# FFN down projection: resident activations loaded in half-width blocks, element-wise sums issued 4 to 11 units ahead

## The reference

```
def conv_ffn(h, w_up, conv_w, conv_b, w_down):
    u = h @ w_up                      # 1024 -> 2 * 2816
    u = centred width-3 depthwise convolution of u over tokens + conv_b
    g, val = jnp.split(u, 2, axis=-1)
    return (jax.nn.silu(g) * val) @ w_down      # 2816 -> 1024

x = x + g_f * f                       # f = conv_ffn(...), in layer()
```

## Time and profile before

| | us |
|---|---|
| median of three runs | 3349.37 |
| profiled execution: its own time | 3348.12 |
| profiled execution: span from first to last instruction | 3346.3 |
| PE busy in the span | 3166.0 (95%) |
| VectorE busy | 2230.3 (67%) |
| ScalarE busy | 1449.4 (43%) |
| down projection of layer 0 | from 1493.5 |
| down projection of layer 1 | from 3063.3 |

### The profile page before, as it was taken

How to read it: one execution, slowest core, us unless ns; L and a number is a source line. 1 busy time by engine, 2 the same in 40 slices (tenths; PEclk the granted TensorE clock), 3 DMA queues, 4 the chain that set the end, 5 groups by cost and what they waited for, 6 DMA issues and landing times. The chain is left out here.

```text
span 3346.3 us, 51277 instructions
## 1 busy us (share of the span) xinstructions
PE 3166.0 (95%) x20077; PEld 2922.7 (87%) x20077; DVE 2230.3 (67%) x3110; ACT 1449.4 (43%) x2665; POOL 985.3 (29%) x748
## 2 busy tenths in 40 slices
PE   6899999997989999999997999999898999999998
PEld 4788788886889999999997878787698999999998
DVE  5555566655166878777973566666518777877895
ACT  3344444444233333334553556665514333334453
POOL 1122222222346434420033122222136544442000
PEclk9999999998999999999999999999899999999999
DMA  6333344333222222239662111111332222225864
GB/s 237 106 102 110 106 124 117 98 103 137 95 70 66 79 73 66 73 106 326 201 189 69 42 31 33 29 30 38 120 114 71 66 73 72 73 73 167 283 202 159
DMA packets 287964, 362.09 MB, mean 108 GB/s; under 512 B 38836, under 2 KB 214061, under 8 KB 286573
## 3 DMA queue, kind: packets, MB, share of 16 engines
q1 hardware_dynamic: 268205, 294.06, 27.9%
q10 hardware_dynamic: 11664, 42.47, 3.9%
q0 software_dynamic: 7856, 22.29, 1.9%
HBM read 277.74 MB, written 67.37 MB: 103 GB/s over the span
## 5 line engine op out<-in xcount | busy, mean ns | idle before, releaser
L198 PE MATMUL psum<-Hh,wh 128*128 128x384 f32 x2048 | 706.8, 345 | 43.5 <-PEq L1018 12.5
L200 PE MATMUL psum<-Hl,wh 128*128 128x384 f32 x2048 | 692.6, 338 | 0.0
L199 PE MATMUL psum<-Hh,wl 128*128 128x384 f32 x2048 | 692.3, 338 | 0.0
L198 PEld LDWEIGHTS psum<-Hh,wh 128*128 128x128 f32 x2048 | 390.1, 190 | 58.6 <-issue 34.1
L1670 DVE SCALAR_TENSOR_TENSOR ff_c<-ff_u,par,ff_c 128x1153 f32<-128x1153 f32 x176 | 401.4, 2281 | 6.1
L199 PEld LDWEIGHTS psum<-Hh,wl 128*128 128x128 f32 x2048 | 390.3, 191 | 0.0
L200 PEld LDWEIGHTS psum<-Hl,wh 128*128 128x128 f32 x2048 | 389.6, 190 | 0.0
L1402 POOL TENSOR_TENSOR wl<-wr,wh 128x1024 fp32r<-128x1024 f32 x88 | 235.4, 2675 | 202.4 <-ACT wh L1201 202.4
L1402 POOL TENSOR_TENSOR ff_dl<-ff_dr,ff_dh 128x1024 fp32r<-128x1024 f32 x76 | 202.1, 2661 | 301.3 <-ACT ff_dh L1201 301.3
L2499 DVE TENSOR_REDUCE da_nb<-psum 128x1 f32<-128x1152 f32 x144 | 174.7, 1233 | 63.3 <-PE psum L2440 63.3
L3085 PE MATMUL psum<-ident,ga_e 128*128 128x128 f32 x1168 | 169.7, 286 | 22.8 <-ACT ga_e L2907 20.9
(11 more groups left out here) (342 smaller groups left out, 7615.9 us busy)
## 6 DMA issues: line engine op xcount, KB each, us to landing
wr<-w_up SPq DMA_DIRECT2D x88, 512.0 KB, 3.8
ff_dr<-w_down SPq DMA_DIRECT2D x130, 256.0 KB, 3.5
wr<-w_down SPq DMA_DIRECT2D x112, 256.0 KB, 3.6
act_save<-ff_c SPq DMA_DIRECT2D x44, 512.0 KB, 2.6
da_mw<-mod_w ACTq DMA_DIRECT2D x40, 512.0 KB, 3.9
wr<-mod_w ACTq DMA_DIRECT2D x40, 512.0 KB, 4.8
ff_c<-act_save SPq DMA_DIRECT2D x88, 192.0 KB, 3.8
wr<-w_qkv_diff SPq DMA_DIRECT2D x24, 512.0 KB, 18.3
```

The costliest lines, as they stand in the source:

```text
L198: pe.matmul(out, w_hi, m_hi, start=start, stop=False)
L199: pe.matmul(out, w_lo, m_hi, start=False, stop=False)
L200: return pe.matmul(out, w_hi, m_lo, start=False, stop=stop)
```

## The change

Three things change. The resident rows are loaded as blocks of 192 KB, in another order: blocks n = 1 of rows 4, 5, 6, 7 at step 7, of rows 0 to 3 and 8 to 10 at steps 17 to 23; blocks n = 0 of rows 0 to 10 at steps 24 to 29 (two in a step); blocks n = 0 of rows 11 to 21 at steps 30 to 40; blocks n = 1 of rows 11 to 21 at steps 45 to 55. Before the first block of the second and of the fourth group SP waits until the 11 blocks of the group before on the same semaphore have landed. P1 begins when the 11 blocks n = 1 of rows 0 to 10 are there. Then, the weight sum of unit q is issued in iteration q - 4 in place of q - 2, and the token sum in iteration q - 3 (P5), q - 6 (P6), q - 11 (P7) or q - 9 (P4). Last, the counts that ACT and DVE wait for follow the new order of sums (SUM_AT), and P2 waits for all blocks of rows1.

```diff
-ROWS_AT = {3: 4, 5: 5, 7: 6, 9: 7, 17: 0, 18: 1, 19: 2, 20: 3, 21: 8, 22: 9, 23: 10, 24: 11, 25: 12, 26: 13, 27: 14, 28: 15,
-           29: 16, 30: 17, 31: 18, 32: 19, 44: 20, 45: 21}
+ROWS_AT = {}
+for i, (row, n) in enumerate([(r, 1) for r in (4, 5, 6, 7, 0, 1, 2, 3, 8, 9, 10)]):
+    ROWS_AT[(4, 5, 6, 7, 17, 18, 19, 20, 21, 22, 23)[i]] = [(row, n)]
+for i in range(HALF):
+    ROWS_AT[24 + i // 2] = ROWS_AT.get(24 + i // 2, []) + [(i, 0)]
+    ROWS_AT[30 + i] = [(HALF + i, 0)]
+    ROWS_AT[45 + i] = [(HALF + i, 1)]
...
+W_LEAD, T_LEAD = 4, {"P5": 3, "P6": 6, "P7": 11, "P4": 9}
+SUM_ORDER = sorted([(q - W_LEAD, 0, q) for q in range(UNITS_DN) if down_name(q) in W_SUMS]
+                   + [(q - T_LEAD[down_name(q)], 1, q) for q in range(UNITS_DN) if down_name(q) in T_SUMS])
+SUM_AT = counted([(tokens, q) for _, tokens, q in SUM_ORDER])
...
-            def load_row(row):
+            def load_block(row, n):
                 done = (b.rows0, b.rows1)[row >= HALF]
-                if row < 2 * KC:
-                    if row % KC < 4:
-                        sp.wait_ge(b.dk, 8)
-                    else:
-                        sp.wait_ge(b.mm, MM_AT[LAST, "P4"])
-                    sp.dma_start((g.raw_h, g.raw_l)[row // KC][:, row % KC, 0:2 * NB], g.act_save[row, :, 0:2 * NB]).then_inc(done, 16)
-                    return
-                sp.wait_ge(b.conv, 3 * 2 * FC)
+                if (row, n) in ((0, 0), (HALF, 1)):
+                    sp.wait_ge(done, 16 * HALF)
+                if row >= 2 * KC:
+                    sp.wait_ge(b.conv, 3 * 2 * FC)
+                elif row % KC < 4:
+                    sp.wait_ge(b.dk, 8)
+                else:
+                    sp.wait_ge(b.mm, MM_AT[LAST, "P4"])
                 sp.wait_ge(stored[row % 2], 32 * (row // 2 + 1))
-                for n in range(2):
-                    sp.dma_start(block(row, n), g.act_save[row, :, n * NB:(n + 1) * NB]).then_inc(done, 16)
+                sp.dma_start(block(row, n), g.act_save[row, :, n * NB:(n + 1) * NB]).then_inc(done, 16)
...
             for q in range(4, UNITS_DN):
-                if q + 2 < UNITS_DN:
-                    unit_sums(q + 2)
+                for at, tokens, j in SUM_ORDER:
+                    if at == q:
+                        (token_sum if tokens else weight_sum)(j)
                 unit_low(q)
```

More of the change, by code:

```diff
@@ L766 @@
 W_SUMS, T_SUMS = ("P5", "P6", "P3", "P7"), ("P5", "P6", "P7", "P4")
+W_LEAD, T_LEAD = 4, {"P5": 3, "P6": 6, "P7": 11, "P4": 9}
+SUM_ORDER = sorted([(q - W_LEAD, 0, q) for q in range(UNITS_DN) if down_name(q) in W_SUMS]
+                   + [(q - T_LEAD[down_name(q)], 1, q) for q in range(UNITS_DN) if down_name(q) in T_SUMS])
+SUM_AT = counted([(tokens, q) for _, tokens, q in SUM_ORDER])
 def sums_through(q, tokens=False):
-    names = [down_name(i) for i in range(q + 1)]
-    return sum((n in W_SUMS) + (n in T_SUMS) for n in names) - (names[-1] in T_SUMS and not tokens)
+    return SUM_AT[int(tokens), q]
 def ring_place(q):
@@ L1148, in _ @@
                     load_back(X_BACK_AT[q])
[L1149 to L1153, removed]
+                for at in (range(8) if q == 7 else (q,) if q > 7 else ()):
+                    for row, n in ROWS_AT.get(at, ()):
+                        load_block(row, n)
                 if nx and q in (98, 100):
@@ L1280, in act_hi @@
                     act.wait_ge(b.rows0, 16 * HALF)
+                elif name == "P2":
+                    act.wait_ge(b.rows1, 2 * 16 * HALF)
                 act.activation(t_high_of(q), t_raw(q), ACT.Copy).then_inc(b.dn_hi, 1)
@@ L1709, in unit_low, with weight_sum @@
                 act_lo(q)
-            def unit_sums(q):
+            def weight_sum(q):
                 i, k = DOWN_UNIT[q]
@@ L1723, in unit_sums, with token_sum @@
                     dve.tensor_tensor(out, first, second, op).then_inc(b.dn_sum, 1)
+            def token_sum(q):
+                i, k = DOWN_UNIT[q]
+                name = DOWN[i]
                 if name in T_SUMS:
@@ L1726, in unit_sums @@
                     dve.wait_ge(b.dn_lo, 2 * (DOWN_FIRST[DOWN.index(before)] + k) + 2)
-                    dve.wait_ge(*((b.rows0, 16 * HALF) if name == "P5" else (b.rows1, 16 * (FC - HALF + 6))))
+                    dve.wait_ge(*((b.rows0, 2 * 16 * HALF) if name == "P5" else (b.rows1, (2 if name == "P4" else 1) * 16 * HALF)))
                     if name in ("P6", "P4"):
```

## The result

The changed kernel takes 3361.38 us (median of 7 runs, 3358.41 to 3366.60) against 3349.59 (7 runs, 3346.62 to 3353.62) for the kernel before: a ratio of 1.0033 with a 95% interval of 1.0024 to 1.0042. It is slower, by 11.8 us where a gain of 2.6 was predicted, and it lies above the range.

What follows compares the result with a forecast made beforehand. The DMA queue, then DVE, was taken to bound the stage. T at 1550.5 against break-even 1551.8 gains 1.3 us a layer, 2.6 in two: 3348.1 becomes 3345.5, or 3346.8 on the median; range 3341 to 3354.

Steps and rivals of the forecast that it cites:

- the part of this change that costs: P7's token sums pulled into iterations 55 to 65, where DVE had been gaining on PE at 1.67 us a unit.
- T: Moment when DVE can start unit 33's weight sum, at its second weight load's landing; forecast 1550.5, before 1558.61, break-even 1551.8.
- the slow bound: Worst case for T, with loads at 343 GB/s: 1553.6, against 1548.9 at best.
- DVE's work behind T, 85.5 us: DVE's sums, low parts and additions from iteration 29 to 65, so unit 65 starts at about T + 85.5.
- P1's wait goes: At unit 22, P1's blocks land by 1533.1 to 1536.0, before PE finishes unit 21 at about 1540.5.
- SP's issues are no bound: After step 24's wait, SP's 24 DMA issues take 11.5 to 16.6 us beside 13.3 of transfer.
- unit 9's weights would land 1.0 us earlier: Four blocks replacing three rows at step 7 save 0.39 MB, so these weights land at 1511.5.
- my slow rate: 343 GB/s for the loads up to P1's last block: 8.39 MB in 24.5 us.
- 13.3 to 15.1 us from the restart to T: After step 24's wait, 13 blocks, 9 weights and unit 33's second load, 5.18 MB at 389 to 343 GB/s.
- rival B: Slower: the load path with its new wait replaces P1's wait, T = 1556.4, 9.2 us in all, 3358.6; chance 0.08.
- weights have 4 iterations (8.6 us) to spare: At step 45, if SP's wait does not hide, the weights it delays still have this slack.
- the larger lead helps no one: Sums issued earlier, 5.4 us more DVE work up to unit 65, bring no gain since a full engine cannot be ahead.

Runs made afterwards that it cites:

- e1_loads_alone: The changed kernel with every sum 2 ahead again, so only the new loads remain against the kernel before; 3345.03 us, ratio 0.9987.
- e4_drain_on_before: The kernel before with one wait more: SP waits in step 24 until rows 0 to 10 have landed; 3356.17 us, ratio 1.0019.
- e3: The changed kernel with each of the four groups of blocks on its own semaphore, so SP does not wait in steps 24 and 45; 3352.87 us.
- e7: The changed kernel without SP's waits in steps 24 and 45 and with all sums 2 ahead; 3338.53 us, ratio 0.9964.
- e8: The changed kernel without the drains, all sums 2 ahead, first halves of rows 11 to 21 issued from step 34 instead of 30; 3339.62 us.
- e10_last_x_back_later: The changed kernel with the sixth and last 768 KB load of x issued in step 78 instead of 75; 3359.19 us, ratio 1.0028.
- e9_later_x_back: The changed kernel with the fifth 768 KB load of x issued in step 70 instead of 64; 3360.57 us, ratio 1.0035.
- e5_weight_lead: The changed kernel with token sums back to 2 ahead and weight sums kept 4 ahead; 3354.57 us, ratio 1.0016.

## Why the prediction was wrong

All medians side by side (the one of 3368.4 has rows 20 and 21 loaded earlier as well):

| loads | sums 2 ahead | sums 3 to 11 ahead |
|---|---|---|
| of the kernel before | 3349.6 | 3368.4 |
| of the change | 3345.0 | 3361.4 |
| of the change, without the drains | 3338.5 | 3352.9 |

Down the columns and along the rows: the leads cost 19, 16 and 14 us, the drains 6.5 and 8.5, the new order of loads, once it has no drains, gains 11 and 15.5. What the prediction called the part of this change that costs is the one that does; what was set against it, an earlier T, was too small by far.

From T to unit 65 the stages are alike to a tenth, and this parts the two terms cleanly: 78.75 to 78.78 us in the six down projections with the old leads of the kernel before, e1_loads_alone and e4_drain_on_before, 80.79 in both with the token sums ahead, 83.5 and 83.6 with the weight sums ahead, and 85.9 to 86.0 in the seven with both leads and no late wait on the way. What differs up to there between executions of one kernel is T, and with both leads a late wait or none.

**The step that failed is the loads' part of the sum: T.** The prediction had it between 1548.9 and 1553.6, which is 55.4 to 60.1 in stage time, and took 57.0. The changed kernel has 63.1 and 61.3, and all twelve down projections traced with these loads and the drain lie past the slow bound (61.2 to 63.8). Two terms of it were too small, the landing of unit 9's weights and the restart of the queue behind the drain; without the drain T is 58.5 to 59.5 (four down projections). Against 57.0 T is 6.1 and 4.3 us late, 10.4 of the 14.4 us between forecast and result.

**Right: DVE's work behind T, 85.5 us.** From 1554.84 to unit 65's start at 1641.77 are 86.9 us, of which 0.95 is the new wait at 1607.70: 86.0. Layer 1 has 85.9. So were the mechanism, T plus all work up to the unit with no lead, and that unit (65).

**Right: P1's wait goes; SP's issues are no bound.** Unit 22 has no wait. SP stood 6.2 us where some 8 were foretold, and the next block landed 2.4 us after its issue, as the earlier trace rows had it. But PE was to be 2.8 us ahead at unit 22, and was 1.1 in layer 0 and nothing in layer 1.

**Wrong: unit 9's weights would land 1.0 us earlier (18.0 in stage time).** In ACT's timeline of the changed kernel

```profile
1511.30 0.63 ACT L1272 ACTIVATE ff_dh<-ff_dr 128x512 fp32r<-128x512 f32 x1 [3.04 <-DMA ff_dr<-w_down]
```

they come 0.5 us later in stage time than in the earlier trace rows (19.55 against 19.06). One pair of traces is not enough here. In the 18 down projections traced with the new loads they come between 18.6 and 19.7, 19.1 in the mean; in the six with the old ones between 19.0 and 20.4, 19.6 in the mean. So about 0.5 us was won, half of what I had taken by 0.39 MB less at 389 GB/s. The bytes alone do not set the time there. The first line is the kernel before, the second the changed one, from the first row or block issued to the landing of the last of the first three rows or four blocks:

```profile
1501.77:1507.75 5.98, 5.98 (x35) 5.77 (x34) 3.37 (x7) 0.00 (x0) 0.00 (x0) 1.00 0.97 315
...
1500.01:1506.04 6.03, 6.03 (x35) 5.84 (x34) 3.35 (x7) 0.00 (x0) 0.00 (x0) 1.00 0.92 283
```

Four blocks (0.79 MB) take as long as three rows (1.18 MB), and 315 GB/s have become 283. Both stretches also hold other transfers, a store of 576 KB issued just before and a load of x; what sets the time was not tried. From there on my slow rate was right. Up to P1's last block it took 1535.88 - 1511.21 = 24.7 us (24.5 predicted at 343 GB/s).

**Wrong: 13.3 to 15.1 us from the restart to T.** It took 1554.82 - 1538.24 = 16.6 (in all twelve down projections with this drain 15.8 to 17.4, with the first landing 2.4 us behind its issue). The stretches: the wait for the first landing, then two parts up to T.

```profile
1535.88:1538.24 2.36, 2.36 (x15) 2.36 (x15) 1.74 (x4) 2.29 (x5) 0.00 (x0) 1.00 0.57 168
1538.24:1547.74 9.50, 9.50 (x57) 9.50 (x56) 4.34 (x8) 3.24 (x7) 0.00 (x0) 1.00 0.96 326
1547.74:1554.82 7.08, 7.08 (x42) 7.08 (x41) 1.32 (x3) 5.23 (x10) 0.00 (x0) 1.00 1.01 359
```

After the first landing the queue runs at 326 GB/s for nearly 10 us. The run without a drain moved 377 and 381 at this place. It is not this trace alone: the 9.5 us behind the first landing have 296 to 327 GB/s in the twelve, and 350 and 331 in e4_drain_on_before. The kernels with blocks and no drain (e3, e7 and e8, both layers) have 379 to 384 in that part of the stage. I had charged the drain its 2.5 us of silence and then a full queue. Its price has a second part, the restart: 5.18 MB at 379 GB/s would be 13.7 us, so 2.9 of the 16.6 belong to it. (An estimate, as the two rates are from two kernels.) These two errors in layer 0, 1.5 us at unit 9 and 1.5 past the slow bound here, make T 63.1 where the slow bound was 60.1. So T fell where rival B had it (62.9 in stage time), by luck and not by B's mechanism: SP issued the load that T waits for at 1548.45, 6.4 us before it landed, so SP was not what held the loads.

**Wrong: weights have 4 iterations (8.6 us) to spare.** I used it as cover for the wait in step 45, which indeed cost nothing: SP's waits from 1560 to 1640 are all for DVE's low parts. But with sums 4 ahead of their unit both weight loads are needed that much earlier, and what is left does not cover a load that lands 7.6 us after its issue behind x. That is DVE idle for 0.95 and 2.57 us in layer 0, 1.28 and 1.61 in layer 1. The prediction's line "the larger lead helps no one" had the gain right and missed this price. On PE it is about 1 us up to unit 65 in layer 0; of the waits behind that, PE's lead over DVE took most, and between units 65 and 74 it lost 0.4 and 0.8.

**The sum again, with measured terms**, layer 0 in stage time: T 63.1 + 85.9 of work + 0.95 of wait = 149.95, against 143.84 before: 6.1 late, 0.4 more by unit 74. Layer 1: 61.3 + 85.9 = 147.2 against 144.1, 3.1 late, 0.8 more by unit 74. Layer 1's other 1.6 us come behind unit 116: from its start to the last matmul are 13.6 us, and 12.0 in the kernel before. This slip comes and goes: e1_loads_alone and e10_last_x_back_later have it as well (13.7 and 13.8), e7_no_drain_old_sums and e9_later_x_back have not (12.0 both), and so it is not the change's. What sets it is open.

## To carry over

When an engine is the bound for a long stretch, work that is moved ahead within it is paid in full. If the first piece of it waits for a load, everything that the engine used to do while that load was under way is paid as well (two pairs of low parts and two additions in e5_weight_lead, 3.4 of its 4.8 us). Count what lies behind that point unit by unit, and ask at which unit the consumer has no lead: a sum of costs is wrong by whatever lead was there.

A wait on landed transfers in the thread that issues the loads cost more than its silence here: price the ramp behind it by the stretch after the trace's own restart, and look for a way to tell the transfers apart (a semaphore for each group) instead of draining.

## What the runs showed of the hardware

A DMA queue that had been drained needed several microseconds to reach its rate again. The view of the DMA traffic from 1536 to 1548.5 of the changed kernel, in 40 slices of 0.31 us (busy share in tenths, then GB/s):

```profile
DMA  0029899767779888997999989999999999999998
GB/s 0 0 59 182 300 320 349 180 210 226 216 210 310 306 305 298 326 297 254 277 280 287 328 338 372 385 375 385 393 410 385 395 402 400 382 393 393 369 346 334
```

From the fourth slice on the engines are busy for six tenths and more, yet they move 180 to 349 GB/s up to the 24th, 7.5 us into the stretch, and only then mostly 370 to 410. All fourteen drains in step 24 that were traced show such a stretch (296 to 350 GB/s over 9.5 us, against 379 to 384 without a drain). A queue that is empty is not always slow, though. At step 7 of the kernel before the queue starts from nothing with a store of 576 KB and then the first rows; the first 1.2 us from 1501.77 on move 301 to 438 GB/s, and slices of 82 to 274 come only behind them. Why the transfers are slow while the engines are called busy was not tried, and it stays open.

Transfers of 192 KB, with weights of 256 KB among them, were as fast as those of 384 KB once the queue was full: 377 and 381 GB/s without the drain, against 354 and 387 in the earlier trace rows.
